# One bias row, added by a vector instruction or by a one-row matmul

## The reference

```python
def chunked_spatial_gating(u, v, ln_g, ln_b, w_s, b_s):
    vn = layer_norm(v, ln_g, ln_b).reshape(B, nc, CHUNK, GMLP_GROUPS, GMLP_GROUP_DIM)
    w = jnp.where(causal[None], w_s, jnp.zeros_like(w_s))
    mixed = jnp.einsum('gts,bcsgd->bctgd', w, vn) + b_s.T[None, None, :, :, None]
    return u * mixed.reshape(B, S, GMLP_WIDTH)
```

## Time and profile before

| | us |
|---|---|
| median of 3 runs (1258.09 to 1260.19) | 1259.28 |
| the profiled execution | 1258.09 |
| its span, first to last instruction | 1256.3 |
| PE busy with matmuls | 1064.4 (85%) |
| DVE busy | 838.5 (67%) |
| ACT busy | 435.4 (35%) |
| POOL busy | 406.5 (32%) |

### The profile page before, as it was taken

The page is one execution under the profiler, slowest core; times in us unless marked ns, Lnnn a source line. Parts: engine busy times, 40 slices in busy tenths (PEclk is TensorE's granted clock), DMA queues, the critical chain, the costliest instruction groups (busy, mean ns, idle before and its releaser), DMA issues.

```text
span 1256.3 us, 18965 instructions
## 1 busy us (share of the span) xinstructions
PE 1064.4 (85%) x7644; PEld 996.1 (79%) x7644; DVE 838.5 (67%) x1754; ACT 435.4 (35%) x907; POOL 406.5 (32%) x344
## 2 busy tenths in 40 slices
PE   1789987798989987878787788878999998899997
PEld 1789987788888887778777787777898786898785
DVE  6779878855676666667776676556654656744756
ACT  4543833122222212221122212211556443455542
POOL 3354003432343343333343343332300163400251
PEclk8899988799999999898999998889999999999999
DMA  9875357999999999999999999998653554454450
GB/s 333 314 278 184 152 176 281 421 420 420 420 420 422 420 420 420 421 421 421 420 421 420 422 420 421 420 421 339 234 196 120 218 198 141 148 183 167 154 183 34
DMA packets 60375, 390.88 MB, mean 311 GB/s; under 512 B 6784, under 2 KB 8832, under 8 KB 16512
## 3 DMA queue, kind: packets, MB, share of 16 engines
q0 software_dynamic: 36864, 268.45, 51.4%
q1 hardware_dynamic: 21808, 120.10, 26.2%
q10 hardware_dynamic: 1616, 1.12, 0.3%
HBM read 388.60 MB, written 1.05 MB: 310 GB/s over the span
## 4 chain that ended last, share of the span: by engine, by line
PE 45%; DMA 35%; DVE 8%; ACT 6%; issue 2%; POOL 2%; SPq 0%; DVEq 0%; ACTq 0%; POOLq 0%
DMA low_pairs<-in_peer_uv,work 20%; DMA rows<-in_peer_uv,work 13%; PE aux L1343 12%; PE pj L1155 5%; PE pj L1157 5%; PE pj L1156 5%; PE aux L1322 4%; PE pj L1419 4%; PE pj L1421 4%; PE pj L1420 4%; ACT whi L599 2%; POOL wlo L606 2%; DMA rows<-in_w_ada 2%; DVE rows L1525 1%; DMA rows<-in_gate_rows 1%
## 5 line engine op out<-in xcount | busy, mean ns | idle before, releaser
L1343 PE MATMUL aux<-work,low_pairs 128*128 128x128 f32 x2304 | 281.7, 285 | 59.5 <-ACT work L1012 59.5
L1343 PEld LDWEIGHTS aux<-work,low_pairs 128*128 128x128 f32 x2304 | 274.7, 200 | 66.3 <-ACT work L1012 66.3
L1343 PE MATMUL aux<-work,rows 128*128 128x128 f32 x1792 | 222.4, 288 | 53.6 <-ACT work L1012 53.6
L1343 PEld LDWEIGHTS aux<-work,rows 128*128 128x128 f32 x1792 | 217.0, 203 | 58.7 <-ACT work L1012 58.7
L783 POOL DMA_INDIRECT low_pairs<-in_peer_uv,work x144 | 135.9, 944 | 217.7 <-PE aux L1343 214.9
L783 POOL DMA_INDIRECT rows<-in_peer_uv,work x112 | 109.8, 981 | 255.9 <-PE aux L1343 177.6
L1155 PE MATMUL pj<-xh,whi 128*128 128x256 f32 x552 | 161.5, 293 | 33.9 <-DVE wlo L551 22.8
L606 POOL TENSOR_TENSOR wlo<-wring,whi 128x1024 fp32r<-128x1024 f32 x34 | 85.7, 2530 | 265.7 <-ACT whi L599 265.7
L606 DVE TENSOR_TENSOR wlo<-wring,whi 128x1024 fp32r<-128x1024 f32 x74 | 104.6, 1437 | 82.1 <-ACT whi L599 81.8
L1156 PE MATMUL pj<-xl,whi 128*128 128x256 f32 x552 | 159.0, 288 | 0.0
L1157 PE MATMUL pj<-xh,wlo 128*128 128x256 f32 x552 | 158.9, 288 | 0.0
(11 more groups left out here) (241 smaller groups left out, 1540.8 us busy)
## 6 DMA issues: line engine op xcount, KB each, us to landing
wring<-in_w SPq DMA_DIRECT2D x80, 1024.0 KB, 4.8
rows<-in_w_ada SPq DMA_DIRECT2D x40, 512.0 KB, 6.3
low_pairs<-in_w_ada SPq DMA_DIRECT2D x1, 4096.0 KB, 13.4
low_pairs<-in_peer_uv,work POOLq DMA_INDIRECT x144
work<-in_late_rows SPq DMA_DIRECT2D x2, 1024.0 KB, 9.6
xT<-in_norm_rows SPq DMA_DIRECT2D x2, 1024.0 KB, 8.3
rows<-in_gate_rows SPq DMA_DIRECT2D x2, 1024.0 KB, 6.9
rows<-in_peer_uv,work POOLq DMA_INDIRECT x112
```

Source lines behind the costliest of these rows:

```text
L1343: ins = mm(peer_sum[t][:, c * P:(c + 1) * P], pair(n)[:, D + c * P:D + (c + 1) * P], diag[:, n % PICKS, :], start=(n % (EXPERT_HEADS * PIC ...
```

## The change

The bias row stays in one partition instead of being copied to 128, and it is added by PE: after each of the eight 128x128 products of `mixed`, a second matmul with one row (a row of ones as the stationary operand, the bias row as the moving one) adds to the same PSUM columns. DVE's additions go, and its multiplication by `ug` reads PSUM directly. The wait for the load moves from DVE to PE.

```diff
-        brow = w4.take(LAYERS * GROUP_ROW).rearrange("p (l n) -> p l n", l=LAYERS)
+        brow = w4.take(LAYERS * GROUP_ROW)[0:1].rearrange("o (l n) -> o l n", l=LAYERS)
...
-                        load_rows(brow.rearrange("p l n -> p (l n)"), "brow", 0, brow_loaded)
+                        sp.dma_start(brow.rearrange("o l n -> o (l n)"), a["brow"]).then_inc(brow_loaded, 16)
...
+                if l == 0:
+                    pe.wait_ge(brow_loaded, 16)
                 for t in range(NT):
                     pe.wait_ge(vn_ready, l * NT + (t + 1))
                     for g in range(4):
-                        ins = mm(aux[:, 4 + t, g * P:(g + 1) * P], vg[:, t, g * P:(g + 1) * P], wsT[:, l * 4 + g, :], start=True, stop=True)
+                        o = aux[:, 4 + t, g * P:(g + 1) * P]
+                        mm(o, vg[:, t, g * P:(g + 1) * P], wsT[:, l * 4 + g, :], start=True, stop=False)
+                        ins = mm(o, ones[0:1, :], brow[:, l, g * P:(g + 1) * P], start=False, stop=True)
                     ins.then_inc(mixed, 1)
...
-                dve.wait_ge(brow_loaded, 16)
                 for t in range(NT):
                     dve.wait_ge(mixed, l * NT + (t + 1))
-                    chain.mark(v.tensor_tensor(zg[:, :, tile_of(t)], by_chunk(aux[:, 4 + t, :]), by_chunk(brow[:, l, :]), ALU.add))
-                for t in range(NT):
-                    chain.wait(back=NT - 1 - t)
-                    v.tensor_tensor(ug[:, :, tile_of(t)], zg[:, :, tile_of(t)], ug[:, :, tile_of(t)], ALU.mult).then_inc(yg_ready, 1)
+                    v.tensor_tensor(ug[:, :, tile_of(t)], by_chunk(aux[:, 4 + t, :]), ug[:, :, tile_of(t)], ALU.mult).then_inc(yg_ready, 1)
```

## The result

| | before | after |
|---|---|---|
| median of 5 runs each, us | 1260.19 (1258.09 to 1263.01) | 1270.06 (1266.65 to 1270.72) |
| profiled execution, us | 1258.09 | 1264.54 |
| its span | 1256.3 | 1262.8 |
| last dot product of the peer stage | 878.03 | 876.50 |

The ratio is 1.0073, with a 95% interval of 1.0056 to 1.009: the change costs 7 to 11 us. The forecast was 1.4 us more, inside a range that ends at 1262.8. In that one the last dot product comes at 879.75: where the peer stage ends moves by some 3 us between executions, so its coming 1.5 us earlier in this table, close to the 1.6 of the forecast, is luck and no measure of the load.

The account below looks back on a forecast made before the run. Transfers were taken to bound the peer stage, and PE's waits, then PE alone, the second block's layers. Profiled 1258.09 - 1.6 (load) + 3.0 (PE) = 1259.5; median 1259.28 + 1.4 = 1260.7 us, range 1255.0 to 1262.8.

Parts of the forecast that it names:

- 1.4 us more: Whole kernel: 1.6 us saved and 3.0 lost, predicted median 1259.28 + 1.4 = 1260.7 us, 0.1% slower.
- The load: Peer stage: shrinking the bias load from 512 KB to 4 KB shortens gaps between 1 MB picks, saving 1.6 us.
- DVE's additions: Second block: dropping two additions (1.19 us) starts piece 32's multiplication 1.2 us earlier a layer if PE is never late.
- A change of height: PE in `mixed`: each switch between one-row and 128-row matmuls adds 0.195 us, sixteen a layer, 3.12 us.
- PE's addition is then 1.79 + 3.12 = 4.91 us a layer: `mixed`: 16 more records at 0.112 us give 1.79; sixteen changes of height give 3.12.
- the lateness of 1.5 us: PE at piece 32: next pass starts 3.7 us late, later idle stretches and restarts absorb 2.2, leaving 1.5 a layer.
- the 3.0 us for two layers: Second block: PE's 1.5 us lateness at piece 32 repeated in both layers, 2 x 1.5.
- the rivals: One-row matmuls cost as others (chance 0.23), height change costs half (0.07), load was hidden (0.12), height change costs twice (0.08).
- The dearest one: Rival on PE in `mixed`: a change of height costs 0.4 us, 3.1 more a layer, giving 1266.9 us; chance 0.08.

Follow-up runs that it names:

- no_add: Kernel before with the bias left out: DVE's four additions dropped, multiplication reads PSUM, PE and the 512 KB load unchanged; 1258.9 us beside 1260.86, ratio 0.9986.
- no_add_small: Kernel before with the bias additions left out and the bias row loaded into one partition, 4 KB; 1257.01 us beside 1260.91, ratio 0.997.
- full_height: Changed kernel with the added matmuls at 128 rows (constant 1/128 against the row broadcast by the 512 KB load); 1257.82 us beside 1260.0, ratio 0.998.
- grouped_2: Changed kernel with one 512-column one-row matmul per token tile, the two side by side, all products kept; 1258.21 us beside 1260.86, ratio 0.9973.
- pe_alone: Kernel before plus PE's alternating one-row matmuls; DVE still adds the row, load still broadcast; 1270.97 us beside 1260.91, ratio 1.008.
- spread: Changed kernel with the pairs placed singly behind weight pieces of the gate's first two passes, the last two adjacent; 1262.21 us beside 1260.86, ratio 1.0009.
- after_2: Changed kernel run again, unaltered, for a second profile; 1270.73 us beside 1260.86, ratio 1.0076, profiled execution 1270.65.
- apart: Changed kernel with its pairs split into two blocks of four, a full gate pass between them; 1264.59 us beside 1260.0, ratio 1.0035.
- half: Changed kernel with four alternating pairs for token tile 0, then four products and one 512-column one-row matmul for tile 1; 1263.0 us beside 1260.91, ratio 1.0018.
- load_back: Changed kernel with the 512 KB load broadcast to 128 partitions again, PE reading partition 0; 1272.39 us beside 1260.0, ratio 1.0095.

## Why the prediction was wrong

The direction of each of its steps holds, and most sizes; what failed is a step that isn't in it.

- *The load* (forecast 1.6 us less, bounds 0 and 1.25): the gaps shrink by 1.24 us here and by 1.29 between no_add and no_add_small, so it is the bytes at the picks' rate, the prediction's lower figure. It isn't hidden: 1.25 us of it stand in the chain up to the second block in all profiles. The gap that the 1.6 was taken from shrinks by 0.62 only.
- *DVE's additions* (1.2 us a layer, if PE is on time): confirmed in no_add (1.1 and 1.4), full_height (1.2 and 1.4) and grouped_2 (1.15 and 1.3). Worth nothing with a late PE: confirmed by pe_alone.
- *A change of height* (0.195 us, sixteen in a layer): confirmed. The pair takes 0.83 us where one product took 0.22; the second layer's pairs, all but the last record at full clock, take 6.59 us against 6.7; and spread, which has all sixteen changes at full clock, loses 1.46 and 1.50 us in the chain's stretches against a forecast of 1.5.
- *What failed*: "PE's addition is then 1.79 + 3.12 = 4.91 us a layer", and with it the lateness of 1.5 us, took the full clock for granted; the 3.0 us for two layers in the sum follow from it. The sixteen drains in a row bring the granted clock down to 1.2 GHz, which stretches the last pairs and the first ten or so matmuls of the pass behind. In the two profiles 1.8 to 5.1 us of clock are lost in a layer. Of the changed kernel's profiled sum, the stretches give 4.45 + 2.98 = 7.4 us in place of 3.0, of which 3.0 are drains (as in spread) and 4.4, what is left, the clock; in after_2 it is 4.4 + 5.85 = 10.3 us, of which 7.3 are the clock. With 1.2 us for the load that is about what the medians show, 9.2 us by the ratio.
- None of the rivals covered it. The dearest one, twice the price for a change, had the right sign and the wrong mechanism. That the kernel came out slower, as forecast, is no merit of the sum: its 1.4 us were within the spread of the runs, and what made the difference plain isn't in it.

The Trainium skill says that TensorE's clock is granted by its activity and falls back when the engine is idle (TensorE: Matmul & The Clock Gate, Part 1). The traces agree that it falls, but show it here with no idle time ahead of it: PE is drawn busy in all 6.00 us from 975 to 981. The drawn busy time doesn't tell work from the extra spacing at a change. The number of records does: from 977.24 to 982.13 there are 24 records of 128 columns in 4.9 us, where before 16 of them took 1.95. Whether this lower rate of work is what brings the clock down is not shown; no run varied it by itself.

What stays open: how dense the drains must be. Pairs with 1.4 us of full work between them (spread, all but the last two) didn't make it fall in either layer of its one profile, of the six blocks of four profiled in apart and half two did, and all eight blocks of eight did (two layers each of after, after_2, load_back and pe_alone). When in a block it falls differs between executions.

## What to carry to other kernels

Adding a row by a one-row matmul is cheap only if it changes the height of the operands rarely: gather the one-row matmuls in one block of as many columns as the bank takes, or give them full height (a constant 1/128 against a broadcast row). Alternated with full-height ones, each change costs about 0.2 us, and a series of them can cost the clock as well, which hits work that isn't part of the change. Before counting instructions at a row's spacing, look for a row where the same two shapes follow each other, and then ask what the stretch as a whole does to the granted clock.

## What the runs showed of the hardware

- A change between 128-row operands and one-row ones costs the same 0.19 to 0.20 us each way as one between 128 and 64 rows: a pair of both takes 0.83 us in place of 0.22 for one and 0.45 for two of full height.
- The granted clock fell with no idle time of PE in the profile (975 to 990, busy 15.00 of 15 us). At 1.2 GHz the same pair takes 1.44 us (983.38 to 984.82), and 512-column records stand 0.43 us apart instead of 0.23.
- The same kernel's falls differ from one execution to the next: in the changed kernel's second layer 1.8 us of clock are lost in one profile and 5.1 in the other, which is 2.9 us in the chain's stretch. The whole time is no measure of it, since the kernel before spreads over 5 to 6 us too (1258.33 to 1263.49, 1258.84 to 1264.83); only half spreads over more, 9 us.
- A transfer of 512 KB into 128 partitions, issued between gathers of 1 MB, delayed the chain by 1.25 us, its bytes at the rate of the gathers (1 MB in 2.49 us).
